# Attention scores in one full-precision product, and rotary tables that carry the tokens' factors, in a two-block transformer kernel

## The reference, cut to what matters

```
h = rmsnorm(x, norm_mix[layer])
# layer 0, forget heads: scores plus differences of a running sum of log gates
s = einsum('bqhd,bkhd->bhqk', qb, k) * scale
s = s + cq[..., :, None] - cum[..., None, :]
# layer 0, chunked heads: s = einsum(q, k) * scale + bias
# layer 1, stick-breaking heads
z = einsum('bqhd,bkhd->bhqk', qb, k) * scale
a = where(mask, exp(log_sigmoid(z) + suffix), 0)
...
# second block
def apply_rope(x, cos, sin):
    x1, x2 = x[..., :half], x[..., half:]
    return concatenate([x1 * cos - x2 * sin, x2 * cos + x1 * sin], axis=-1)
dq, dk, nq, kc, k_sel, k_win = each apply_rope(u @ w_in part)
```

## Time and profile before

| | |
|---|---|
| median of 3 runs | 2130.88 us (2129.32 to 2131.18) |
| the profiled execution | 2129.74 us, span 2127.9 us |
| PE busy | 2043.0 us, 96% of the span |
| PEld, DVE, ACT, POOL busy | 76%, 47%, 43%, 41% |
| mean granted clock of TensorE | 0.985 of full speed |

### The profile page before, as it was taken

How to read it: one execution, slowest core, us unless ns; L and a number is a source line. 1 busy time by engine, 2 the same in 40 slices (tenths; PEclk the granted TensorE clock), 3 DMA queues, 4 the chain that set the end, 5 groups by cost and what they waited for, 6 DMA issues and landing times. The chain is left out here.

```text
span 2127.9 us, 28756 instructions
## 1 busy us (share of the span) xinstructions
PE 2043.0 (96%) x9996; PEld 1619.3 (76%) x9996; DVE 999.3 (47%) x1600; ACT 915.1 (43%) x1783; POOL 871.1 (41%) x648
## 2 busy tenths in 40 slices
PE   8999999999999978899999998998999999999997
PEld 6777788888887755688888886766667888888886
DVE  7545545322355678542312264777555553323133
ACT  5555443332344654442323355655554343223234
POOL 3223345444454221254444453542113555544454
PEclk9999999999999999999999998999999999999999
DMA  4222132232222110122322222221101332322223
GB/s 145 74 76 80 60 99 91 97 99 99 94 94 89 50 40 30 40 92 97 99 99 95 92 99 70 90 91 49 40 32 62 98 99 90 98 99 98 93 96 109
DMA packets 50582, 177.89 MB, mean 84 GB/s; under 512 B 5536, under 2 KB 5800, under 8 KB 50480
## 3 DMA queue, kind: packets, MB, share of 16 engines
q1 hardware_dynamic: 48096, 172.07, 24.5%
q10 hardware_dynamic: 2384, 4.43, 0.6%
HBM read 174.36 MB, written 2.12 MB: 83 GB/s over the span
## 5 line engine op out<-in xcount | busy, mean ns | idle before, releaser
L457 POOL TENSOR_TENSOR w_lo<-raw,w_hi 128x512 fp32r<-128x512 f32 x644 | 870.9, 1373 | 1239.7 <-ACT w_hi L1061 1239.5
L1061 ACT ACTIVATE w_hi<-raw 128x512 fp32r<-128x512 f32 x644 | 370.9, 623 | 830.2 <-PE gemm_banks L484 811.1
L482 PE MATMUL gemm_banks<-h_hi,w_hi 128*128 128x512 f32 x1512 | 615.4, 407 | 7.4 <-POOL w_lo L457 7.2
L484 PE MATMUL gemm_banks<-h_hi,w_lo 128*128 128x512 f32 x1512 | 593.7, 393 | 0.0
L483 PE MATMUL gemm_banks<-h_lo,w_hi 128*128 128x512 f32 x1512 | 593.5, 393 | 0.0
L482 PEld LDWEIGHTS gemm_banks<-h_hi,w_hi 128*128 128x128 f32 x1512 | 285.1, 189 | 89.6 <-issue 28.2
L482 PE MATMUL gemm_banks<-u_hi,w_hi 128*128 128x512 f32 x848 | 330.3, 390 | 4.1 <-POOL w_lo L457 2.9
L484 PEld LDWEIGHTS gemm_banks<-h_hi,w_lo 128*128 128x128 f32 x1512 | 285.2, 189 | 62.9
L484 PE MATMUL gemm_banks<-u_hi,w_lo 128*128 128x512 f32 x848 | 329.9, 389 | 0.0
L483 PE MATMUL gemm_banks<-u_lo,w_hi 128*128 128x512 f32 x848 | 329.9, 389 | 0.0
L483 PEld LDWEIGHTS gemm_banks<-h_lo,w_hi 128*128 128x128 f32 x1512 | 285.8, 189 | 56.8 <-issue 2.6
(11 more groups left out here) (323 smaller groups left out, 1964.5 us busy)
## 6 DMA issues: line engine op xcount, KB each, us to landing
raw<-slabs SPq DMA_DIRECT2D x322, 512.0 KB, 3.2
table<-rel_rows ACTq DMA_DIRECT2D x4, 512.0 KB, 3.9
x<-x_t SPq DMA_DIRECT2D x4, 256.0 KB, 6.7
x<-x_t ACTq DMA_DIRECT2D x4, 256.0 KB, 6.9
cos<-pos SPq DMA_DIRECT2D x2, 256.0 KB, 10.3
y_t<-x SPq DMA_DIRECT2D x2, 256.0 KB, 2.8
y_t<-x ACTq DMA_DIRECT2D x2, 256.0 KB, 2.7
y_t<-x SPq DMA_DIRECT2D x1, 512.0 KB, 2.8
```

The costliest lines, as they stand in the source:

```text
L457: pool.tensor_tensor(w_lo[:, j, part], raw[:, j, part], w_hi[:, j, part].bitcast(F32), ALU.subtract).then_inc(slab_split, 1)
L482: pe.matmul(out, high, rhs_hi, start=first, stop=False)
L484: return pe.matmul(out, low, rhs_hi, start=False, stop=last)
L1061: act.activation(w_hi[:, m % 2, part], raw[:, m % 2, part], ACT.Copy).then_inc(slab_hi, 1)
```

## The change

1. In layer 0 and in the stick-breaking half, q and k stay whole in float32 (`q_t`, `k_t`, in the place of the four rounded tiles). DVE writes them straight from the bank. ACT's rounding copies, DVE's subtractions and their semaphores are gone. The scores are one float32 matmul per head; the forget product before them stays in float32r, and so does the mask's product in stick-breaking steps.
2. In the second block, the cosine and sine tables are once multiplied by `rstd`. A rotated tile is taken out by two instructions from the bank, one times the cosines straight into its place, one times minus the sines into `tmp`; ACT swaps the latter into another part of `tmp` (two parts each, used in turn), and DVE adds it.
3. The swaps move on ACT behind the exponentials (odd halves) or behind the scaling by shares (even halves), the additions on DVE behind `take` or behind the step's combination. ACT waits for a finished rotation only ahead of the windows of kc.
4. Mask and zeroing for the second block move into the second layer's MLP, the zeroing of `pcT` to half 4, and the eight scalings of x from steps 5 to 12 into the merge loop behind the attention.

```
@@ PE, scores(s), the same in cd_scores(s)
-                    pe.wait_ge(qk_split, 2 * (p + 1))
+                    pe.wait_ge(gemm_free, done["k", p])
...
-                parts = ((q_hi, k_hi), (q_hi, k_lo), (q_lo, k_hi))
-                for n, (q, k) in enumerate(parts):
-                    for head in range(2):
-                        rows = slice(HEAD * head, HEAD * (head + 1))
-                        last = pe.matmul(SC[:, 2 * b + head, 0:w], q[rows, p % 2, i * P:w], k[rows, p % 2, 0:w],
-                                         start=(n == 0 and p >= 4), stop=n == 2, skip_group_check=True)
...
+                for head in range(2):
+                    rows = slice(HEAD * head, HEAD * (head + 1))
+                    pe.matmul(SC[:, 2 * b + head, 0:w], q_t[rows, p % 2, i * P:w], k_t[rows, p % 2, 0:w],
+                              start=(p >= 4), stop=True, skip_group_check=True).then_inc(scored, 1)
@@ ACT
-                            act.wait_ge(gemm_free, c.gemm.at())
-                            dst = q_hi if name == "q" else k_hi
-                            act.activation(dst[:, p % 2, :], tmp[:, "qk".index(name), :], ACT.Copy).then_inc(qk_hi, 1)
...
             def e_late(name, p):
-                if name in ROTATED:
-                    act.wait_ge(rope_ready, E_ROPE[name, p])
                 if name == "kc":
-                    windows(tmp[:, 2, :], 0)
+                    act.wait_ge(rope_ready, E_ROPE["kc", 0])
+                    windows(sq_e[:, :], 0)
...
+            def e_swaps(h):
+                for name, p, turn in ends_of(h):
+                    if name in ROTATED:
+                        n = E_ROPE[name, p]
+                        act.wait_ge(gemm_free, taken_out[name, p])
+                        if n > 2:
+                            act.wait_ge(rope_ready, n - 2)
+                        for r in range(0, P, 32):
+                            o = r ^ 32
+                            last = act.activation(tmp[r:r + 32, 2 + n % 2, :], tmp[o:o + 32, n % 2, :], ACT.Copy)
+                        last.then_inc(swapped, 1)
...
             for h in range(-E_AHEAD, 0):
                 e_half(h)
+                e_swaps(h)
...
                     weigh(E_BASE + s, e_step(s)[3])
+                if s > 0:
+                    e_swaps(2 * s - 1)
                 e_half(2 * s)
...
+                e_swaps(2 * s)
                 e_half(2 * s + 1)
@@ DVE
+            for table2 in (cos2, sin2):
+                link(dve.tensor_tensor(table2[:, :], table2[:, :], rstd[:, :], ALU.mult))
...
-                    dve.scalar_tensor_tensor(tmp[:, 2, :], tmp[:, 0, :], scale, cos2[:, :], ALU.mult, ALU.mult)
-                    link(dve.scalar_tensor_tensor(tmp[:, 3, :], tmp[:, 1, :], scale, sin2[:, :], ALU.mult, ALU.mult))
-                    dve.tensor_tensor(dst, tmp[:, 2, :], tmp[:, 3, :], ALU.add).then_inc(rope_ready, 1)
+                    dve.tensor_tensor(dst, dst, tmp[:, 2 + n % 2, :], ALU.add).then_inc(rope_ready, 1)
...
-                    last = dve.tensor_tensor(tmp[:, 0, :], bank, rstd[:, :], ALU.mult)
+                    scale = QK_SCALE if name in ("q", "nq") else 1.0
+                    dve.scalar_tensor_tensor(tmp[:, E_ROPE[name, p] % 2, :], bank, -scale, sin2[:, :], ALU.mult, ALU.mult)
+                    last = dve.scalar_tensor_tensor(rotated(name, p), bank, scale, cos2[:, :], ALU.mult, ALU.mult)
...
                 if s >= 1:
                     e_take(s - 1)
+                e_rotated(2 * s - 1)
                 if s < E_STEPS:
                     e_shares(s)
                 e_half(2 * s + 1)
                 if s < DIFF_STEPS:
                     e_combine(s)
-                if 5 <= s < 5 + KT:
-                    j = s - 5
-                    dve.scalar_tensor_tensor(x[:, j, :], x[:, j, :], gains_of("final1")[:, j:j + 1], rstd_in[:, :],
-                                             ALU.mult, ALU.mult)
+                e_rotated(2 * s)
```

More of the change, by code:

```diff
@@ L767, in cd_scores @@
                 if i == 0:
[L768 to L776, removed]
+                    pe.wait_ge(gemm_free, done["k", p])
+                for head in range(2):
+                    rows = slice(HEAD * head, HEAD * (head + 1))
+                    pe.matmul(SC[:, 2 * b + head, 0:w], q_t[rows, p % 2, i * P:w], k_t[rows, p % 2, 0:w], start=False,
+                              stop=True, skip_group_check=True).then_inc(scored, 1)
             def cd_flip(s):
@@ L1396, in e_end @@
             def e_end(name, p):
-                if name in ROTATED:
-                    swap()
-                elif name == "tk":
+                if name == "tk":
                     act.wait_ge(gemm_free, c.gemm.at())
@@ L1429, in e_half @@
                             gemm_slab()
+                        taken_out[name, p] = c.gemm.at()
                         e_end(name, p)
@@ L1675, in _ @@
             mean(D, rstd, 0)
-            def low_parts(low, high):
-                for name, p, j, n in units(AB_ITEMS, low, high):
-                    if n and j == n - 1 and name in "qk":
-                        k = "qk".index(name)
-                        dve.wait_ge(qk_hi, 2 * p + k + 1)
-                        hi, lo = ((q_hi, q_lo), (k_hi, k_lo))[k]
-                        dve.tensor_tensor(lo[:, p % 2, :], tmp[:, k, :], hi[:, p % 2, :].bitcast(F32),
-                                          ALU.subtract).then_inc(qk_split, 1)
             ab_banks, ab_after = ring(units(AB_ITEMS, KT, 8 * len(AB_ITEMS)), 1 - c.gemm.slot)
@@ L1794, in _ @@
                     mixed((s - 5) // 4)
-                if s >= 1:
-                    low_parts(*half(s - 1, 1))
                 evacuated(*half(s, 0))
@@ L1801, in _ @@
                     shares(s)
-                low_parts(*half(s, 0))
                 evacuated(*half(s, 1))
@@ L1872, in _ @@
                 latent(Q_TILES + j, j == 0, acc2)
-            def cd_low_parts(low, high):
-                for name, p, j, n in units(CD_ITEMS, low, high):
-                    if name in "qk" and j == n - 1:
-                        k = "qk".index(name)
-                        dve.wait_ge(qk_hi, 16 + 2 * p + k + 1)
-                        hi, lo = ((q_hi, q_lo), (k_hi, k_lo))[k]
-                        dve.tensor_tensor(lo[:, p % 2, :], tmp[:, k, :], hi[:, p % 2, :].bitcast(F32),
-                                          ALU.subtract).then_inc(qk_split, 1)
             cd_banks, cd_after = ring(units(CD_ITEMS, 0, 1000), c.gemm.slot)
@@ L1992, in _, with second_block @@
             add_out(gains_of("mlp1"))
-            mlp(gain2, more=True)
+            def second_block(j):
+                if j == 1:
+                    wide_mask(sin1, "causal")
+                if j == 3:
+                    dve.memset(kcmp[:, :], 0.0)
+                    link(dve.memset(V_cmp[:, :], 0.0))
+            mlp(gain2, more=True, beside=second_block)
             mean(D, rstd_in)
@@ L2127, in e_half @@
                 for name, p, turn in ends_of(h - 1):
-                    e_second(name, p)
+                    if name not in ROTATED:
+                        e_second(name, p)
                 for name, p, turn in ends_of(h):
```

68 lines of the change are left out of this document (22 added, 46 removed).

## The result

The changed kernel takes 2111.37 us (median of 4 runs, 2108.83 to 2116.85), the kernel before 2130.1 (median of 4): the ratio is 0.9918, 95% interval 0.9902 to 0.9934. Forecast were 2114, range 2103 to 2128. Measured again with five rounds the changed kernel took 2110.26 (2108.94 to 2113.61), ratio 0.9911 (0.9898 to 0.9925). Its profiled execution took 2108.83 us, span 2107.0, so 20.9 us less than that of before where the medians differ by 18.7; that trace is the fastest of the four. Two executions are far slower than all others and stand in no ratio: 4601.18 us of the kernel before beside the first four experiments, and 7096.77 us of own_swap_odd.

The account below looks back on a forecast made before the run. TensorE is busy nearly throughout, so only its own work, waits and lower clock count. +6.1 - 1.2 - 5.8 - 2.0 - 10.1 - 4.0 = -17.0 from 2129.74 us: 2112.7, as median 2114, range 2103 to 2128.

Parts of the forecast that it names:

- TensorE, +6.1: First block's scores: one full-precision product costs PE more than three rounded ones, +6.1 us over twelve head pairs.
- First scores, -1.2 and -1.4: First score of layer 0 and first stick score: waits for the keys' low part shrink by 1.2 and 1.4 us.
- Stick-breaking steps, -4.4: Three stick-breaking steps: without ScalarE's rounding, Abs begins 1.5 us earlier in each, -4.4 us.
- The clock, -2.0 and -4: A third of lower-clock losses regained: -2.0 us in stick-breaking steps, -4 at the second block's start and last steps.
- Start of the second block, -2.1: Second block's start: the slab PE waits for is split about 2.1 us earlier, -2.1 us.
- Term (a): Second block's attention, from 1471.65 us: waits for turned shares behind swaps shrink by 1.8, 0.6 and 1.2 us, -3.6.
- Term (b): Second block's attention at 1407.65 us: PE's wait of 3.22 us for turned shares goes, -3.2 us.
- rival (1): Waits give way to others, the clock stays, only a third of 17.1 us is won: 2131 us; chance 0.14.
- Term (c): Second block's attention: compressed branch's key tile is ready 1.2 us earlier, so ScalarE may split a slab sooner, -1.2 us.
- (2): Rival: ScalarE's new order hurts, swaps between exponentials and shares cost 26 us over eight tiles: 2147 us; chance 0.05.
- (3): Rival: two heads no longer run side by side in full precision after a rounded product: 2149 us; chance 0.02.
- (4): Rival: busy times are right, the single score form is cheaper, -9.6 in place of +6.1: 2098 us; chance 0.05.

Follow-up runs that it names:

- own_swap_odd: The changed kernel, but VectorE itself swaps the rows of all six tiles ending in odd halves from 11 on; 2114.43 us (median of the other five), ratio 0.9926.
- stick_copies: The changed kernel, but ScalarE still copies each q and k in the stick-breaking steps, into a tile nobody reads; 2116.32 us, ratio 0.9935.
- masks_back: The changed kernel, but mask and zeroing stand again on VectorE right ahead of the second block's first tile; 2114.86 us, ratio 0.9931.
- late_swaps: The changed kernel, but five odd-half tiles are swapped on ACT behind the scaling by shares and added at the step's end on DVE; 2117.17 us, ratio 0.9942.
- own_swap_ks: The changed kernel, but VectorE itself swaps the rows of the one tile ending in half 19 (ks); 2112.47 us, ratio 0.9915.

## Why the prediction was right

**Total.** Forecast -17.0 on the profiled execution, measured -20.9 and, in a second trace, -19.4 by span; by medians -18.7. Every group of terms had the right sign, but the total is nearer than its parts, and that is luck. Of 17.1 us of waits that were to go, PE's idle time shows 10.4 (84.9 to 74.5 us). For the clock 6.0 were counted, and it gave some 14: PE's busy time fell by 10.5 us although the scores cost 3.9 more. (Busy time is modelled, so this is an estimate; the mean granted clock over the span, 0.985 before and 0.993 now, bounds it at 0.015 x 2127.9 - 0.007 x 2107 = 17.) What the waits gave too little the clock gave too much, and the scores were cheaper than forecast.

**TensorE, +6.1: too large by 2.2.** A plain pair costs 0.31 us to the next product, as forecast (2.96 against 2.65), and 0.34 from its first score to that of the next pair. A forget pair costs 0.30, not 0.9. The step that failed is "that 0.10 now is paid by the forget group and stays, so the three products cost only 2.65 - 0.40": full precision gains the same 0.10 behind the forget group (0.95 in place of 1.05 us at 512 keys), so it cancels, and the change of mode inside a step shows no cost of its own. 8 x 0.34 + 4 x 0.30 = 3.9. Layer 0 grew by 1.93 behind its first score, less than its eight pairs cost, since a wait at 215 us fell from 1.03 to 0.35.

**First scores, -1.2 and -1.4.** In layer 0 1.23 us became 0.35: the score now waits for the table of the forget gates. In the stick steps the whole 2.33 went, where only rounding, subtraction and hand-overs, 1.4, had been counted.

**Stick-breaking steps, -4.4.** The three waits fell by 1.9, 1.5 and 1.5 us, and stick_copies shows the cause. One was partly given back: behind 758.96 the next transposes wait 2.16 us where they waited 1.14.

**The clock, -2.0 and -4: the term that was mis-sized.** "I count a third" was a guess between bounds, and too low. By the same sum as in the prediction the stick stage lost 6.3 us and now loses 0.02 x 115.9 = 2.3; the start lost 5.2 and now nothing; the sparse steps lost 6.6 and now 0.02 x 159 = 3.2. That is 4.0 and 8.6 us. The latent half behind the stick steps, for which nothing was counted, lost 0.04 x 96 = 3.8 and now 0.9. These are upper bounds, since part of it lay in PE's waits. masks_back is the clean measure: 1.7 us more of waits, 4.0 us more of time.

**Start of the second block, -2.1.** The stage gave -4.80 us in every trace with the change at the start. The wait for the slab fell by 2.4 (4.3 to 1.92), as forecast, but the next one, for VectorE's `VT`, grew from 1.48 to 2.27: 1.6 by the waits and 3.2 by the clock.

**Attention steps. Term (a), -3.6: its waits gave -2.1.** At the first place 3.67 us became 0.44 and 1.57, so -1.7 where 1.8 was forecast; at the second 3.25 became 2.38, -0.9 where 0.6 was. The third, -1.2, failed: its swap did move behind the scaling, and the shares come sooner, but the compressed scores need the whole rotated query and now wait 2.04 us for it, where 1.66 was waited for the shares. The hand count followed the shares only. Steps 13 to 47 gave -6.6 in all: also a wait of 1.04 us at 1451 that went, and the clock.

**Term (b), -3.2 at 1407, failed:** steps 10 to 13 are 0.4 us shorter. The wait went, as the prediction said, and 3.44 us for a slab took its place one step on. The prediction set the swap between the exponentials and that slab's split and counted no cost for it there; late_swaps and own_swap_ks show that the swap is the cause of this wait, and that the stretch gets no shorter without it. From 1307 to 1456 us, where terms (b) and (c) had 4.4 us of waits, PE idled 9.1 us (busy for 139.88 of 149.00), and idles 9.7 now (137.75 of 147.40). This is rival (1) at one place.

**Term (c), -1.2,** can't be read apart from the fetch of instructions, which moves steps 0 to 10 by 1.4 to 2.1 us.

**Rivals.** (1) held for the waits in part: 10.4 of 17.1 us were won, not a third; that the clock stays as it is was wrong. (2) is out as a sum, but not as a mechanism: the waits of 1.57, 2.38 and 2.04 us all stand behind swaps, and moving five of them elsewhere made the kernel 5 to 7 us slower. (3) and (4) are out by the score rows.

## What to carry to other kernels

Price a wait on TensorE by two numbers, its length and what the clock does behind it; a first wait of 4.2 us shortened to 1.9 gave back 4.0 us. Before a wait is counted as won, look at everything that the moved instruction now stands ahead of: here the next slab's split, and a product that needs the tile whole. Add up PE's idle and busy time over the stage, since a wait that fell by its name can come back under another, once even as "issue". And cost two precisions by the distance from the first matmul to the next product on both sides of the change, since what a group gains behind another holds for either.

## What the runs showed that was not expected

A packet of PE's instructions (queue 8, 16 KB) inside a slab's burst makes ScalarE wait 1.8 us longer for the slab (3.32 against 1.53). The Trainium skill, Runtime: NRT & Kernel Launch, Instruction fetch mechanics, says that programs are refilled by blocks of 16 KiB, 256 instructions, and that the cost of crossing one is mostly hidden. The block size agrees with the packets; the cost is not hidden in this stretch, where ScalarE waits for slabs. All 14 traces agree: in the nine in which the packet lies 5.7 to 8.3 us behind step 3's start the wait for that slab is 3.3 to 3.6 us, in the other five 1.3 to 1.6. Why a packet of 16 KB delays a slab of 512 KB by 1.8 us is open.

VectorE's addition of two tiles takes 0.69 us at 1392.18 in the changed kernel and 1.63 at 1393.94 in own_swap_ks, where POOL's subtraction runs beside it (3.23 us for two, 2.52 where it runs alone). The Trainium skill, SBUF — State Buffer, SBUF: two separate sides, says that a VectorE operation with two inputs in SBUF and a GpSimd operation hold a common pair of ports in turn; these rows agree. The scaling of x is one more: in the kernel before seven of the eight ran beside POOL and took 1.76 to 1.79 us, the one at 1392.44 without it 0.74, and in the merge loop of the changed kernel all eight take 0.74 to 0.75. So moved there they cost VectorE 6.0 us and not the 13.1 of the earlier trace rows.
